# Attention's weighted latent sums as split products, with the turned weights leaving PSUM as a rounded and a low part

## What is computed

```python
    _, sel = lax.top_k(score, topk)
    kv_sel = jax.vmap(lambda c, i: c[i])(c_kv, sel)
    s = jnp.einsum('bqhc,bqkc->bqhk', q_lat, kv_sel).astype(jnp.float32) * (ATT_HEAD_DIM ** -0.5)
    valid = sel <= qpos[None, :, None]
    s = jnp.where(valid[:, :, None, :], s, -jnp.inf)
    p = jax.nn.softmax(s, axis=-1).astype(c_kv.dtype)
    return jnp.einsum('bqhk,bqkc->bqhc', p, kv_sel)
...
    o_lat = dsa_attention(q_lat, q_idx, w_idx, c_kv, k_idx)
    y_att = jnp.einsum('bthc,hcd->bthd', o_lat, w_uv).reshape(bsz, t_len, ATT_WIDTH)
```

## Time and profile before

| what | value |
| --- | --- |
| median of 3 runs | 1018.18 us (1017.34 to 1019.1) |
| profiled execution | 1017.49 us, span 1015.8 us |
| PE busy | 996.9 us, 98% of the span |
| DVE busy | 714.0 us, 70% |
| ACT busy | 493.8 us, 49% |
| POOL busy | 118.1 us, 12% |
| the attention stage | about 529.5 to 610 us of the span |

### The profile page before, as it was taken

One profiled execution on the slowest core, in us unless ns is written; L12 is line 12 of the kernel. 1 busy time (PEld: TensorE's weight loads), 2 busy tenths in 40 slices (PEclk: granted clock), 3 DMA queues, 4 the chain that ended last, 5 costly groups with the idle time before them and its releaser, 6 DMA issues.

```text
span 1015.8 us, 18999 instructions
## 1 busy us (share of the span) xinstructions
PE 996.9 (98%) x7028; PEld 907.9 (89%) x7028; DVE 714.0 (70%) x1317; ACT 493.8 (49%) x868; POOL 118.1 (12%) x92
## 2 busy tenths in 40 slices
PE   9999999999999999999999999999999999999996
PEld 8999999999999988699765668889999999988886
DVE  6988888887322264699997523699989889942236
ACT  6656665566121264546346522576656665812121
POOL 0000000001121262045302205320000000000000
PEclk9999999999999999999999999999999999999999
DMA  7233332323223313132110102113323232333212
GB/s 252 84 100 107 102 105 90 116 80 105 86 86 111 113 44 116 36 123 82 44 42 1 43 1 83 43 42 126 124 83 124 85 121 96 125 103 101 98 57 84
DMA packets 30849, 90.48 MB, mean 89 GB/s; under 512 B 4689, under 2 KB 5329, under 8 KB 30801
## 3 DMA queue, kind: packets, MB, share of 16 engines
q1 hardware_dynamic: 30800, 89.83, 26.7%
HBM read 87.72 MB, written 2.10 MB: 88 GB/s over the span
## 4 chain that ended last, share of the span: by engine, by line
PE 81%; DVE 15%; ACT 2%; issue 1%; DMA 0%; SPq 0%; DVEq 0%; ACTq 0%
PE ps L1229 38%; PE ps L1287 22%; PE ps L1152 9%; DVE sc L2201 3%; DVE top L2200 3%; PE ps L1714 2%; PE ps L1424 1%; PE ps L1692 1%; DVE qk L2240 1%; PE ps L1705 1%; DVE wlo L1877 1%; PE ps L1489 1%; PE ps L1722 1%; PE ps L1337 1%; PE ps L1335 1%
## 5 line engine op out<-in xcount | busy, mean ns | idle before, releaser
L1229 PE MATMUL ps<-tsum,whi 128*128 128x264 f32 (+1 forms) x1280 | 243.1, 282 | 0.5 <-ACT ht L790 0.5
L1229 PEld LDWEIGHTS ps<-tsum,whi 128*128 128x128 f32 x1280 | 202.3, 188 | 0.7 <-issue 0.7
L1229 PE MATMUL ps<-tsum,wlo 128*128 128x264 f32 (+1 forms) x640 | 180.3, 282 | 0.0
L1229 PE MATMUL ps<-xh,whi 128*128 128x264 f32 (+1 forms) x480 | 135.4, 282 | 0.3 <-ACT sil L790 0.3
L1229 PE MATMUL ps<-xl,whi 128*128 128x264 f32 (+1 forms) x480 | 135.5, 282 | 0.0
L1229 PE MATMUL ps<-xh,wlo 128*128 128x264 f32 (+1 forms) x480 | 135.3, 282 | 0.0
L729 ACT ACTIVATE whi<-wraw 128x1408 fp32r<-128x1408 f32 (+1 forms) x48 | 74.6, 1555 | 123.0 <-PE ps L1287 123.0
L1787 DVE TENSOR_TENSOR wlo<-wraw,whi 128x1408 fp32r<-128x1408 f32 (+1 forms) x38 | 70.0, 1843 | 85.3 <-ACT whi L729 85.3
L1287 PE MATMUL ps<-hh,whi 128*128 128x264 f32 (+1 forms) x462 | 124.2, 323 | 0.0
L1287 PE MATMUL ps<-hh,wlo 128*128 128x264 f32 (+1 forms) x462 | 123.5, 322 | 0.0
L1287 PE MATMUL ps<-hl,whi 128*128 128x264 f32 (+1 forms) x462 | 123.4, 321 | 0.0
(11 more groups left out here) (287 smaller groups left out, 1828.0 us busy)
## 6 DMA issues: line engine op xcount, KB each, us to landing
wraw<-in_ffn_w_gate SPq DMA_DIRECT2D x43, 512.0 KB, 4.2
wraw<-in_ffn_w_up SPq DMA_DIRECT2D x42, 512.0 KB, 4.3
wraw<-in_ffn_w_down SPq DMA_DIRECT2D x32, 384.0 KB, 3.2
wraw<-in_ffn_w_down SPq DMA_DIRECT2D x32, 320.0 KB, 3.5
wraw<-in_w_in SPq DMA_DIRECT2D x19, 512.0 KB, 4.5
wraw<-in_w_out SPq DMA_DIRECT2D x8, 512.0 KB, 4.4
out<-zrow SPq DMA_DIRECT2D x8, 256.0 KB, 2.0
x<-in_x SPq DMA_DIRECT2D x3, 528.0 KB, 7.5
```

Source lines behind the costliest of these rows:

```text
L1229: mm = pe.matmul(ps[:, bank, 0:(HT, HALF_SEQ)[p // 2]], w[:, k * P:(k + 1) * P], v[:, k, :], start=(first and k == 0 and n == 0), stop=(k ...
```

## The change

The weighted sum becomes three products of `float32r` parts. A turned tile leaves PSUM twice: ACT writes the rounded part for every tile (`weights_hi`, in place of `copy_odd`), and behind it DVE writes the turned tile less that part (`weights_lo`, in place of `copy_even`). Two sets of buffers (`pt_h`, `pt_l`) alternate; the buffers overlay the mLSTM values that are dead by then, and the fourth score buffer moves to another tensor. ACT also rounds all latents once (`chi`), after the copy of the turned latents, and POOL subtracts (`split_latents`) after the weight unit `mix_lo(9)`.

The meta tile has only 16 keys. It is turned with 32 rows, its low part is written 32 partitions below the rounded part, and `meta_c` holds the rounded latents at both places with zeros between, so that one product over 64 partitions gives both products with the rounded latents; a second over 16 partitions adds the low latents.

```diff
@@ tensors
-            cs = sb("cs", [P, NT, 256], F32, s)
+            with ExitStack() as c_scope:
+                cs = sb("cs", [P, NT, 256], F32, c_scope)
+            c_parts = sb("c_parts", [P, NT, 256], F32R, s)
+            clo, chi = c_parts[:, :, 0:LAT], c_parts[:, :, LAT:2 * LAT]
...
+            pts = sb("pts", [P, NT * ML_H * VW], F32R, s)
+            meta_c = sb("meta_c", [64, LAT], F32R, s)
...
-        sbuf = [sil[:, 0, :], sil[:, 1, :], pt_flat[:, 1024:1024 + T], pt_flat[:, 1024 + T:1024 + 2 * T]]
+        sbuf = [sil[:, 0, :], sil[:, 1, :], pt_flat[:, 2048:2048 + T], qk[:, 3, :]]
+        pt_h = [pts[:, e * 512:(e + 1) * 512] for e in range(2)]
+        pt_l = [pts[:, (2 + e) * 512:(3 + e) * 512] for e in range(2)]
@@ POOL, after mix_lo(9)
+                def split_latents():
+                    pool.wait_ge(c_hi, 1)
+                    pool.wait_ge(ct_turned, 1)
+                    pool.tensor_tensor(clo, cmat, chi.bitcast(F32), ALU.subtract).then_inc(c_lo, 1)
+                    m = N_META
+                    link(pool.memset(meta_c[:, :].bitcast(F32), 0.0))
+                    for e, r in enumerate((0, 32)):
+                        pool.wait_ge(c_lo, e + 1)
+                        pool.tensor_copy(meta_c[r:r + m, :], chi[0:m, 0, :].bitcast(F32)).then_inc(c_lo, 1)
+                    pool.wait_ge(c_lo, 3)
@@ ACT
                 act.activation(ct[:, END[3]:T], ps[:, 5, 0:P], ACT.Copy).then_inc(ct_ready, 1)
+                act.activation(chi[:, :, :], cmat, ACT.Copy).then_inc(c_hi, 1)
                 hi(MIX0 + 4, 0, UW, False)
...
-                def copy_odd(G, tiles):
+                def weights_hi(G, tiles):
                     for i in tiles:
                         t = TP0[G] + i
-                        if t % 2 == 1:
-                            act.wait_ge(pt_turned, t + 1)
-                            if t >= 2:
-                                act.wait_ge(pv_step, t - 1)
-                            act.activation(pt_flat[0:ROWS[i], 512:1024], ps[0:ROWS[i], 1, :], ACT.Copy)\
-                                .then_inc(pt_odd, 1)
+                        R = META_ROWS if i == 0 else P
+                        act.wait_ge(pt_turned, t + 1)
+                        if t >= 2:
+                            act.wait_ge(pv_step, t - 1)
+                        act.activation(pt_h[t % 2][0:R, :], ps[0:R, t % 2, :], ACT.Copy).then_inc(pt_hi, 1)
@@ PE
                     if t >= 2:
-                        pe.wait_ge(pt_even if t % 2 == 0 else pt_odd, t // 2)
+                        pe.wait_ge(pt_lo, t - 1)
...
                 def weigh(G, i):
                     t = TP0[G] + i
-                    pe.wait_ge(pt_even if t % 2 == 0 else pt_odd, t // 2 + 1)
-                    if i == 0 and G >= 1:
-                        pe.wait_ge(ol_ready, G)
-                    pe.matmul(ps[:, 3, :], cmat[0:ROWS[i], i, :], pt_flat[0:ROWS[i], (t % 2) * 512:(t % 2 + 1) * 512],
-                              start=(i == 0), stop=(i == 1 + G // 2)).then_inc(pv_step, 1)
+                    if i == 0:
+                        pe.wait_ge(pt_hi, t + 1)
+                        if G >= 1:
+                            pe.wait_ge(ol_ready, G)
+                        pe.wait_ge(c_lo, 3)
+                        m = N_META
+                        pe.matmul(ps[:, 3, :], clo[0:m, 0, :], pt_h[t % 2][0:m, :], start=True, stop=False)
+                        pe.wait_ge(pt_lo, t + 1)
+                        pe.matmul(ps[:, 3, :], meta_c[:, :], pt_h[t % 2][0:64, :], start=False, stop=False).then_inc(pv_step, 1)
+                        return
+                    pe.wait_ge(pt_hi, t + 1)
+                    pe.matmul(ps[:, 3, :], chi[:, i, :], pt_h[t % 2], start=False, stop=False)
+                    pe.matmul(ps[:, 3, :], clo[:, i, :], pt_h[t % 2], start=False, stop=False)
+                    pe.wait_ge(pt_lo, t + 1)
+                    pe.matmul(ps[:, 3, :], chi[:, i, :], pt_l[t % 2], start=False, stop=(i == 1 + G // 2)).then_inc(pv_step, 1)
@@ DVE
-                def copy_even(G, tiles):
+                def weights_lo(G, tiles):
                     for i in tiles:
                         t = TP0[G] + i
-                        if t % 2 == 0:
...
+                        dve.wait_ge(pt_hi, t + 1)
+                        if i == 0:
+                            ins = dve.tensor_tensor(pt_h[t % 2][32:32 + META_ROWS, :], ps[0:META_ROWS, t % 2, :],
+                                                    pt_h[t % 2][0:META_ROWS, :].bitcast(F32), ALU.subtract)
+                        else:
+                            ins = dve.tensor_tensor(pt_l[t % 2], ps[:, t % 2, :], pt_h[t % 2].bitcast(F32), ALU.subtract)
+                        ins.then_inc(pt_lo, 1)
```

More of the change, by code:

```diff
@@ L98 @@
 DROPS = END[1] - TOPK
+META_ROWS = 32
 def build(nc, a, out):
@@ L184, in build @@
             upad = sb("upad", [P, 4 * (T + CONV - 1)], F32, s)
-            v1 = sb("v1", [P, NT, ML_H, VW], F32, s)
+            with ExitStack() as v_scope:
+                v1 = sb("v1", [P, NT, ML_H, VW], F32, v_scope)
+            pts = sb("pts", [P, NT * ML_H * VW], F32R, s)
+            meta_c = sb("meta_c", [64, LAT], F32R, s)
             sg = sb("sg", [P, 4, T], F32, s)
@@ L398, in build @@
         pt_turned = sem("pt_turned")
-        pt_even = sem("pt_even")
-        pt_odd = sem("pt_odd")
+        pt_hi = sem("pt_hi")
+        pt_lo = sem("pt_lo")
+        c_hi = sem("c_hi")
+        c_lo = sem("c_lo")
         pv_step = sem("pv_step")
@@ L694, in mixer @@
                 mix_lo(9)
+                split_latents()
                 causal_mask(3)
@@ L1103, in attention @@
                             if G >= 1:
-                                copy_odd(G - 1, (0, 1))
+                                weights_hi(G - 1, (0, 1))
                         if (G, half) in HEAD_HI:
@@ L1108, in attention @@
                         j, g = 1 + (G - 1) // 2, (G - 1) % 2
-                        copy_odd(G - 1, range(2, j + 1))
+                        weights_hi(G - 1, range(2, j + 1))
                         act.wait_ge(pv_step, TP0[G])
@@ L1702, in turn @@
                     if t >= 2:
-                        pe.wait_ge(pt_even if t % 2 == 0 else pt_odd, t // 2)
+                        pe.wait_ge(pt_lo, t - 1)
                     for q in range(4):
-                        mm = pe.transpose(ps[0:ROWS[i], t % 2, q * P:(q + 1) * P], pbuf[G % 2][:, q, START[i]:END[i]],
-                                          ident[:, :])
+                        k0, k1 = (START[i], END[i]) if i else (0, META_ROWS)
+                        mm = pe.transpose(ps[0:k1 - k0, t % 2, q * P:(q + 1) * P], pbuf[G % 2][:, q, k0:k1], ident[:, :])
                     mm.then_inc(pt_turned, 1)
@@ L2362, in attention @@
                 late = None
-                def copy_even(G, tiles):
+                def weights_lo(G, tiles):
                     for i in tiles:
                         t = TP0[G] + i
-                        if t % 2 == 0:
-                            dve.wait_ge(pt_turned, t + 1)
-                            if t >= 2:
-                                dve.wait_ge(pv_step, t - 1)
-                            dve.tensor_copy(pt_flat[0:ROWS[i], 0:512], ps[0:ROWS[i], 0, :]).then_inc(pt_even, 1)
+                        dve.wait_ge(pt_hi, t + 1)
[5 more added lines that the diff above has]
+                        ins.then_inc(pt_lo, 1)
                 def late_round(G, place):
@@ L2386, in attention @@
                             if G >= 1:
-                                copy_even(G - 1, (0, 1))
+                                weights_lo(G - 1, (0, 1))
                             late_round(G, 0)
@@ L2393, in attention @@
                     if G >= 1:
-                        copy_even(G - 1, range(2, last_tile + 1))
+                        weights_lo(G - 1, range(2, last_tile + 1))
                         if late is not None:
```

## The result

The changed kernel takes 1032.31 us (median of 4 runs, 1031.06 to 1033.21) where the kernel before took 1017.8 beside it (1017.34 to 1019.1): ratio 1.014, 95% interval 1.0122 to 1.0157, so 14.5 us slower. The prediction said 1027.0 and a range of 1020 to 1032. The direction is right; the median lies 0.3 us above the range, and 5.3 above the predicted time.

A forecast was written before the change was run, and what follows sets the result against it. TensorE is busy 98% of the span, but the ring paces the 400-key stretches and DVE the part ahead. Stage 8.4 + latents' copy 0.6 = 9.0 on 1017.49 gives 1026.5, 1027 against the median; range 1020 to 1032.

The forecast's parts named there:

- TensorE's own work: Weighted sum: three rounded products replace one plain one, saving 0.06 us on 20 tiles and 0.48 on 8 meta tiles, 5.0.
- The walk: Attention stage stepped through by stretch: +2.8 (first four), +2.0, +1.6, +1.7, +0.3 (eighth and ninth), sum 8.4 us; 73%.
- the ring: Attention stage: mask (DVE), exponential (ACT), eviction, weighted sum (PE) set the pace in stretches of 400 keys.
- Every tile evicted twice: Attention stage: 14 more ACT roundings of 0.50 us and 14 more DVE subtractions of 0.62, between nothing and 15.7 us.
- The latents' copy on ACT, +0.6: ACT at 426 us, ahead of a weight unit DVE waits for: 0.6 us goes down DVE's unbroken row to 527.
- the term that I priced at nothing: POOL's latents subtraction after the unit split from 489.5: 1.5 us, hidden by idle time; without that cover at most 3.
- A clock of 1.00 in the stage: Sign expected in the profile after: TensorE's granted clock stays at 1.00 throughout the attention stage.
- rival 3: TensorE's clock falls in the fifth and sixth stretches, 2 to 5 us for each fall: 1029 to 1034; 8%.
- Rivals 1, 2 and 5: 1: TensorE's work decides, 1014, 7%; 2: waits overlap better, 1016 to 1020, 7%; 5: products run unrounded, 1037, 1%.
- Rival 4: Every added eviction in the stage lies on the path: +15.7 - 5.0 + 0.6, 1029.5 us; no separate chance given.

The follow-up runs named there:

- no_low_link: The changed kernel without DVE's subtraction, TensorE's third product repeated with the rounded part, the weights' low part left out: 1013.83 us, ratio 0.9964.
- warm_more: The changed kernel with idle-time matmuls on TensorE at its long waits (12, 9, 5, 5) and nine ahead of the first weighted sum: 1028.95 us, ratio 1.0108.
- chi_late: The changed kernel with ACT's rounding of the latents moved from ahead of a weight unit to the mLSTM part: 1030.51 us, ratio 1.0129.
- lo_behind: The changed kernel with DVE's subtractions for tiles 0 and 1 of a stretch behind the masks of heads 3 and 4: 1031.06 us, ratio 1.0137.
- combo: The changed kernel with early subtractions and late selection rounds behind the masks, and ACT's rounding of the latents late: 1027.36 us, ratio 1.0085.
- before_pool: The kernel before with one more POOL instruction, a 128x640 subtraction of the latents whose result nobody reads: 1017.6 us, ratio 1.0.

## Why the prediction was wrong, step by step

*TensorE's own work: right for the tiles of 128 keys, too low for the meta tile.* A tile of 128 keys takes 0.79 us where its parts are ready (589.34 to 590.13, forecast 0.80) and 1.07 behind a wait (580.95 to 582.02). A meta tile takes 0.85, where I had 0.57, even where TensorE waits for nothing:

```profile
576.01 0.49 PE L1741 MATMUL ps<-pts,c_parts 16*128 16x512 f32 x1
576.43 0.50 PE L1743 MATMUL ps<-pts,meta_c 64*128 64x512 f32 x1
576.86 0.66 PE L1730 MATMUL ps<-ident,qi 128*128 128x128 f32 x4
```

Its two products start 0.42 us apart at full clock, and not 0.23. So TensorE saves 20 x 0.07 + 8 x 0.20 = 3.0 us in the change, and not 5.0. The walk hardly used this term, since it had the ring set the pace. Without the ring's new link the meta tile takes 0.65 (547.84 to 548.49 in `no_low_link`) and the kernel gains 3.7 us, with the 0.5 ahead of the stage still in it.

*Every tile evicted twice: right in size.* Two roundings in a row take 1.05 us and a subtraction 0.68 to 0.69. ACT's 14 more are free, DVE's 28 subtractions carry the cost; the walk rightly had most of it on them.

*The walk: right from the fifth stretch on, too low ahead of it.* Counted from the first latent-query product and with the clock held (`warm_more`), the fifth stretch is 2.2 us longer than before (forecast 2.0), the sixth 1.7 (1.6), the seventh 1.7 (1.7), the eighth and ninth 0.6 (0.3). The first four stretches are 4.5 us longer in `warm_more` and in the change, and 4.1 in `chi_late`; I had 2.8. The 0.4 us between them have two reasons, and neither is the ring. In the change TensorE still works on scores at half clock (547.01, 2.02 us), and the projection at 548.83 starts 0.49 us behind ACT's copy of the sum. In `warm_more` it starts 0.05 behind the copy, but the fillers hold the copy back by 0.4 us. In `chi_late`, which has no fillers and no fall there, neither delay stands. So the ring alone makes 4.1 us, and 1.3 are missing in the walk. One piece of them has a name. In the third stretch DVE normalises a head behind the two subtractions; DVE, then POOL:

```profile
543.58 0.69 DVE L2405 TENSOR_TENSOR pts<-ps,pts 128x512 fp32r<-128x512 f32 x1
544.19 1.86 DVE L2354 TENSOR_SCALAR upad<-upad,mv,mls 128x128 f32<-128x128 f32 x4
...
543.91 1.29 POOL L723 TENSOR_TENSOR xl<-ht,xh 128x512 fp32r<-128x512 f32 x1 [1.68 <-ACT xh L1096]
```

The four instructions took 1.09 us before and take 1.86 here, because the subtractions push them against POOL's instruction. In `lo_behind`, where they run at 540.96 and POOL at 538.05 and 543.24, they take 1.11, and the projection behind them comes 1.6 us earlier, the moved subtractions' share among it. The masks, the exponentials and the copy for which the projection waits (0.58 us in `warm_more`) follow on the four instructions directly, so 0.8 us are this collision. The remaining 0.5 I can't place. The stage with the clock held is 10.6 us longer, 0.4 of them the fillers', and the walk said 8.4.

*The latents' copy on ACT, +0.6: fell.* Alone it costs 0.0. The 0.5 us found at the latent queries come from the term that I priced at nothing, POOL's subtraction: I looked for who needs its result and for POOL's own idle time, and not for who runs beside it.

*A clock of 1.00 in the stage: this is the step that failed.* The sum of the prediction has no term for it; full clock stood in the list of what the profile would show, and rival 3, the clock, had a chance of 8% and two places. The runs show 3.4 us at the medians, and 3.8 if the fillers' 0.4 are added (an estimate). It is the largest of the errors. The second is the walk's first four stretches, 1.3 us without the clock. The range ended 0.3 us below the median, and with either of the two in the sum it would have held it. The clock fell in a wait that the walk had rightly foreseen (3.14 us ahead of tile 9), and also in the third and seventh stretch. Windows of 1 us in the fifth stretch:

```profile
564.00:565.00 1.00, 0.00 (x0) 0.00 (x0) 0.93 (x5) 0.00 (x0) 0.00 (x0) 1.00 0.00 0
565.00:566.00 1.00, 0.00 (x0) 0.00 (x0) 0.71 (x4) 0.94 (x3) 0.00 (x0) 1.00 0.00 0
566.00:567.00 1.00, 0.00 (x0) 0.00 (x0) 0.00 (x0) 0.98 (x3) 0.00 (x0) 0.51 0.00 0
567.00:568.00 1.00, 0.97 (x2) 0.74 (x3) 0.99 (x2) 0.00 (x0) 0.00 (x0) 0.50 0.00 0
```

It fell 2.1 us into the wait and stays at 0.50 until 572, five microseconds after TensorE started again. The Trainium skill (TensorE: Matmul & The Clock Gate, Part 1) states the same: an idle TensorE drops to half clock and gets it back after sustained work. These rows agree. Others show that a wait does not always bring a fall. In the sixth stretch TensorE waited 2.31 us ahead of 580.95, and the clock stayed:

```profile
579.00:580.00 1.00, 0.00 (x0) 0.00 (x0) 0.63 (x3) 0.98 (x3) 1.00 (x1) 1.00 0.00 0
580.00:581.00 1.00, 0.05 (x1) 0.05 (x1) 0.07 (x1) 1.00 (x4) 1.00 (x1) 1.00 0.02 8
```

Rival 3 in its own words, 1029 to 1034, held the result, but by luck in part: it named the fifth and the sixth stretch, and the falls came in the third, fifth and seventh. Still the walk met its condition, so 8% was far too little: a forecast of a 3 us wait should have carried a price for the clock, as a range.

The sum as it should have been: 10.6 for the stage, 0.5 ahead of it, 3.4 for the clock, together 14.5; without the fillers' delay 10.2, 0.5 and 3.8.

*Rivals 1, 2 and 5* fell: the ring has no slack, its waits do not overlap better than in the walk in this order of the work (`combo` shows that another order is shorter), and the products run as rounded ones. Rival 4, every eviction on the path, has the size nearly right (11.3 by its sum) and the reason wrong, since ACT's 14 are free.

## What to carry to other kernels

A second eviction that must follow the first lengthens a ring by its own time and by all that stands behind it on that engine; TensorE's saved products pay for it only where TensorE, and not the ring, sets the pace. When a forecast contains waits of TensorE of a microsecond or more, price its clock as part of the forecast, and as a range: the same waits cost it in one run and not in another. When work is given to POOL, look at which DVE instructions run beside it, not only at who waits for the result.

## What the runs showed of the hardware

- **DVE's TENSOR_SCALAR from SBUF to SBUF is held up beside POOL's subtraction.** At 528 and 400 columns it ended 0.28 to 0.36 us behind POOL's end: 2.95 us instead of 0.49 at 447.60 in `chi_late`, 1.06 instead of 0.49 at 450.31 and 0.88 instead of 0.37 in the change. Of the four of 128 columns at 544.19 the first took 1.09 us instead of 0.34 and ended 0.08 behind. In `before_pool`, where POOL's had only 0.18 us to go, it took 0.41 instead of 0.37 and ended 0.23 behind. DVE's TENSOR_TENSOR from PSUM (543.58, 0.69) and MATCH_REPLACE8 (495.03, 0.56) beside the same POOL instructions keep their time. The Trainium skill (SBUF — State Buffer, SBUF: two separate sides) describes a port pair that an instruction of DVE in a two-port mode and one of POOL take in turn, each for its whole length. The long overlaps agree with that, the short one of `before_pool` fits it poorly; that this instruction used such a mode no row shows.
- **TensorE's clock fell beside waits of 1.11, 1.52 and 3.14 us and not beside one of 2.31.** In the change TensorE was idle from 545.0 to 546.11, and the granted clock was 0.77 from 545 to 546 and 0.50 in the next two microseconds. After the wait of 1.52 us ahead of 592.25 it was 1.00 until 593, 0.66 in the next microsecond and 0.50 in the two after, with TensorE at work. `chi_late` has the same four waits (1.11, 3.13, 2.30 and 1.53 us), and there the clock stayed at 1.00 beside the first and the last, was at 0.50 from 563, within the wait of 3.13, and fell to 0.53 in the microsecond from 580, behind the wait of 2.30. How much is lost differs from run to run: the times of `lo_behind` and `combo` spread over 5.7 and 5.6 us, those of `warm_more`, with the clock held, over 0.4.
- **The meta tile's two products start further apart than those of 128 keys.** At full clock the product over 64 partitions starts 0.42 us behind that over 16 (576.01 to 576.43), that over 32 partitions of `no_low_link` 0.33 (547.84 to 548.17), and the products over 128 partitions 0.23. Why, no run tells.
- **The third product of a tile behind a wait starts 0.38 to 0.39 us behind the second**, not 0.23 (567.29 to 567.68 in `warm_more`). That is the ring and not TensorE: DVE's subtraction for the same tile runs there from 566.93 to 567.62, and the product that reads its result starts 0.06 us later.
